# Where a slot of split weights begins: 192 bytes further for the down products, 128 bytes for the u units

## What is computed

```
merged = sum_i gate_i * (o_i @ w_proj_i);  x = x + merged @ w_out                  # w_out: "down"
x = x + square(relu(h @ w_mlp_in)) @ w_mlp_out                                     # "up", "down"
swiglu(x, w1, w3, w2) = (silu(x @ w1) * (x @ w3)) @ w2                             # four of them: "up", "up", "down"
u, v = split(gelu(x @ sgu_w_in));  out = (u * mix(layer_norm(v))) @ sgu_w_out      # gating stage: u, v "up"; "down"
out = attention(...) @ w_o                                                         # "down"
```

## Time and profile before

| | |
|---|---|
| runs | 1498.37, 1498.73, 1499.16 us; median 1498.73 us |
| profiled execution | 1499.37 us, span of its instructions 1497.5 us |
| TensorE matmul busy | 1445.4 us, 97% of the span |
| TensorE weight loads busy | 1326.4 us, 89% |
| VectorE, ScalarE, GpSimd busy | 62%, 44%, 6% |
| TensorE clock granted | 0.987 of full, mean |
| DMA | 268.43 MB, 179 GB/s |

### The profile page before, as it was taken

One profiled execution on the slowest core, in us unless ns is written; L12 is line 12 of the kernel. 1 busy time (PEld: TensorE's weight loads), 2 busy tenths in 40 slices (PEclk: granted clock), 3 DMA queues, 4 the chain that ended last, 5 costly groups with the idle time before them and its releaser, 6 DMA issues.

```text
span 1497.5 us, 25321 instructions
## 1 busy us (share of the span) xinstructions
PE 1445.4 (97%) x10475; PEld 1326.4 (89%) x10484; DVE 930.4 (62%) x1363; ACT 660.1 (44%) x834; POOL 95.9 (6%) x78
## 2 busy tenths in 40 slices
PE   8989998999999999999999999999999998999997
PEld 6978987899999999999789999999999886799996
DVE  5887457555675555757885555746555767665556
ACT  5655534333444434545244334425334466543342
POOL 0012141000020000100020000100000100100000
PEclk9999998999999999999999999999999999999999
DMA  7443444776568555665356556667555440455551
GB/s 256 150 141 95 146 142 155 219 218 212 193 222 284 185 188 191 198 195 196 113 178 204 187 193 196 198 195 250 179 190 196 147 141 29 141 198 196 196 196 57
DMA packets 191526, 268.43 MB, mean 179 GB/s; under 512 B 5740, under 2 KB 164752, under 8 KB 191182
## 3 DMA queue, kind: packets, MB, share of 16 engines
q1 hardware_dynamic: 186336, 250.05, 51.2%
q0 software_dynamic: 4224, 15.91, 3.2%
q10 hardware_dynamic: 878, 1.21, 0.3%
HBM read 261.92 MB, written 4.19 MB: 178 GB/s over the span
## 4 chain that ended last, share of the span: by engine, by line
PE 84%; DVE 9%; ACT 3%; DMA 2%; issue 1%; POOL 0%; DVEq 0%; ACTq 0%
PE bank L764 82%; DVE split L2024 2%; DMA ring<-in_ffn_w 2%; PE bank L787 2%; ACT split L1553 1%; DVE resid L2101 1%; DVE resid L2109 1%; DVE stats L2080 1%; DVE resid L2078 1%; ACT act_out L1576 0%; DVE arena L2616 0%; DVE stats L2038 0%; DVE arena L2221 0%; ACT gain_rows L1680 0%; DMA resid<-in_x 0%
## 5 line engine op out<-in xcount | busy, mean ns | idle before, releaser
L764 PE MATMUL bank<-hT_hi,split 128*128 128x256 f32 (+1 forms) x3984 | 710.7, 280 | 7.5 <-ACT act_out L1692 5.4
L2024 DVE TENSOR_TENSOR split<-ring,split 128x2048 fp32r<-128x2048 f32 x212 | 484.3, 2286 | 369.1 <-ACT split L1553 363.8
L764 PEld LDWEIGHTS bank<-hT_hi,split 128*128 128x128 f32 (+1 forms) x3984 | 613.8, 189 | 16.0 <-issue 9.8
L1553 ACT ACTIVATE split<-ring 128x2048 fp32r<-128x2048 f32 (+1 forms) x224 | 428.1, 1912 | 352.9 <-PE bank L764 313.7
L764 PE MATMUL bank<-hT_lo,split 128*128 128x256 f32 (+1 forms) x1992 | 556.5, 279 | 0.0
L764 PEld LDWEIGHTS bank<-hT_lo,split 128*128 128x128 f32 (+1 forms) x1992 | 376.3, 189 | 2.0
L764 PE MATMUL bank<-split,hid_hi 128*128 128x512 f32 x992 | 286.2, 395 | 0.0
L764 PEld LDWEIGHTS bank<-split,hid_hi 128*128 128x128 f32 x992 | 183.3, 189 | 37.7 <-issue 0.8
L764 PE MATMUL bank<-split,hT_hi 128*128 128x256 f32 (+1 forms) x896 | 174.1, 294 | 6.5 <-DVE split L2024 4.8
L764 PE MATMUL bank<-split,hid_lo 128*128 128x512 f32 x496 | 158.3, 393 | 0.0
L764 PEld LDWEIGHTS bank<-split,hT_hi 128*128 128x128 f32 x896 | 141.5, 189 | 14.4 <-DVE split L2024 5.4
(11 more groups left out here) (216 smaller groups left out, 964.5 us busy)
## 6 DMA issues: line engine op xcount, KB each, us to landing
ring<-in_ffn_w SPq DMA_DIRECT2D x132, 1024.0 KB, 5.1
ring<-in_w_in SPq DMA_DIRECT2D x19, 1024.0 KB, 5.1
ring<-in_w_mlp_in SPq DMA_DIRECT2D x16, 1024.0 KB, 6.2
ring<-in_w_mlp_out SPq DMA_DIRECT2D x16, 1024.0 KB, 4.9
ring<-in_sgu_w_in SPq DMA_DIRECT2D x16, 1024.0 KB, 5.4
ring<-in_sgu_w_out SPq DMA_DIRECT2D x8, 1024.0 KB, 4.9
ring<-in_kv_w SPq DMA_DIRECT2D x6, 1024.0 KB, 5.4
ring<-in_w_out SPq DMA_DIRECT2D x4, 1024.0 KB, 4.9
```

What stands on the lines that cost most here:

```text
L764: ins = pe.matmul(o, lhsT, rhs, start=start, stop=stop)
L1553: act.activation(halves(q if i is None else q + BODY, n)[0], ring[:, u % SLOTS, 0:n], ACT.Copy).then_inc(hi_ready, 1)
L2024: dve.tensor_tensor(lo, ring[:, u % SLOTS, 0:n], hi.bitcast(F32), ALU.subtract).then_inc(split_ready, 1)
```

## The change

Units of the down products lie 48 floats (192 bytes) further in their slot (at 384 modulo 512 in place of 192), the `su` units 32 floats (128 bytes; at 320 in place of 192). Units of `by_token` keep their 32, all others their 0. The last unit of each down stage lies in `two` and does not move.

```diff
+SHIFTS = {"wout": 3 * SHIFT // 2, "md": 3 * SHIFT // 2, "w2": 3 * SHIFT // 2, "so": 3 * SHIFT // 2, "wo": 3 * SHIFT // 2,
+          "mu": 0, "w1": 0, "w3": 0, "sv": SHIFT, "su": SHIFT}
+
+
 def split_shift(q):
 
-    return SHIFT if by_token(SPLIT_NAMES[q]) else 0
+    name = SPLIT_NAMES[q]
+    if by_token(name) and name[0] != "sv":
+        return SHIFT
+    return SHIFTS.get(name[0], 0)
```

## The result

The change makes the kernel slower: 1509.19 us (median of 5 runs, 1508.76 to 1512.06) against 1498.73 us before (5 runs of the same comparison); the ratio is 1.0075, with a 95% interval of 1.005 to 1.010: small, but clear of the noise. In later comparisons the kernel before had a median of 1496.5 to 1499.4 us over 13 to 29 runs. The profiled execution of the changed kernel took 1512.06 us, with a span of 1510.3.

The account below looks back on a forecast made before the run. It took TensorE's dense matmuls (97% busy) as the bound. Down units (-5.4 us) and su units (-1.6 us), other terms 0, sum to -7.0 us from 1499.37: 1492 us for the median, 8-in-10 range 1481 to 1507.

Parts of the forecast that it names:

- What bounds the kernel: Whole kernel: TensorE's matmuls, busy 97% of the span, bound it, so a nanosecond per matmul goes to the end whole.
- Slot passes at nothing: VectorE's and ScalarE's writing of the slots: costs the same at either shift, and both engines have slack; term 0.
- The su units, -1.6 us: Gating stage: 384 su matmuls go from 117.8 to 113.6 ns, as sv at the same 192 bytes apart; 1.6 us won.
- The down units, -3.3 ns each: 68 down units, 1632 matmuls at about 229 ns: each gets 3.3 ns shorter at offset 384, 5.4 us won.
- The analogy with 256 columns: Down units: the 4.3 ns between sv at shift 32 and memory values at 0 was taken over for 512 columns.
- The up units behind down units, term 0: MLP and FFNs: addresses stay; 7.3 us to win or 12.1 us to lose, nothing to say which, so 0.
- The third rival: Up units lock slow: three fast FFNs run at 117.8 ns, +12.1 us, less 5.4 and 1.6 won: 1504 us; chance 0.18.
- its second price, 1509 us: Three fast FFNs' up units at 117.8 ns, with no gain in the down units: 1509 us.
- more than forecast: Rival: a constant down rhythm makes all following up units fast, 1484 us, or most of 13 ns goes, 1478; chance 0.17.
- It stays at one for a whole stage: TensorE's timeline: the same instruction comes at two or three steady distances (113.6 or 117.8, 229 or 233 ns), one per stage.
- The rule of the Trainium skill: TensorE has two independent SBUF read ports, so no offset would change a distance and the change would be worth 0.
- The first 200 us as before to the nanosecond: Test of the prediction: the first 200 us hold no moved unit, so each distance there must be unchanged.

Follow-up runs that it names:

- the nudge: The changed kernel plus one bf16 matmul of zeros (64 columns), adding nothing, ahead of each FFN chunk's w1 unit from the third chunk on: 1499.07 us, ratio 1.0011.
- the kernel with lo at 64: The changed kernel, with only the down units' first part (hi) at 48 floats and the second (lo) at 64: 1513.45 us, ratio 1.0102.
- the one with 64 floats: The changed kernel, with the down units 64 floats (256 bytes) further in place of 48, at 448 modulo 512: 1492.60 us, ratio 0.9985.

## Why the prediction was wrong

The forecast was 1492 us; the time is 1509.19, beyond the range's 1507.

- *What bounds the kernel* held. Of the 12.8 us by which the profiled span grew, 3.7 arose ahead of the first moved unit and 1.9 in the second attention stage; nearly all of the rest are distances between matmuls.
- *Slot passes at nothing* held: around the first FFN VectorE's took 2293 ns, ScalarE's 1918 ns on average.
- *The su units, -1.6 us*: right in size, -1.7 us in the profile (113.3 ns). The reason given, 192 bytes between the operands as with sv, is not enough: the w1, w3 and mu units at 320, as far from their moving operand, ran at 117.8 behind another stream.
- *The down units, -3.3 ns each*: the sign was right, the size wrong. It was -1.1 ns where the up units were short before and -2.0 where they were long. The even rhythm of the unit in `two` did come (226.7 ns when settled), but each down unit spends its first five matmuls at 227 to 237 ns, behind long and short up units alike. The analogy with 256 columns was worth nothing.
- *The up units behind down units, term 0*: this is the step that failed. They carried the sign. Three FFNs went from 113.6 to 117.8 ns, 4.2 ns x 96 = 0.40 us a chunk, up to 12.1 us in all. In the traces the three FFNs show 8.6 us of it, net of what their down units won, in 8, 9 and 9 pairs of up units. The third rival had this mechanism and its price; what I lacked was its probability. That its second price, 1509 us, is the measured time is luck: it puts the gain of the down units at nothing, which was 1.1 to 2.0 ns a matmul.

And it could have been read from the trace of before. I used the even rhythm of the earlier trace rows for the size of the down term, but did not ask how such a rhythm hands over. In the stages of before with long up units (MLP, third FFN) these were entered at 226 to 227 ns in all 22 hand-overs, in those with short ones at 230 to 231 in all of 26. An even rhythm of 226 to 227 can only leave at 226 to 227. By these rows, to forecast that rhythm was to forecast long up units in every stage, and my rival "more than forecast" had it the wrong way round. They were a hint and no proof: at the old offset long up units and a last distance of 227 may just as well keep each other up.

Smaller points:

- *"It stays at one for a whole stage"* misread the rows. The down unit of 233.3 ns lies between 96 up matmuls at 118.9 ns and the short ones: it is where the first FFN turned.
- *The unit in `two`*: 1.81 us / 8 is 226.3 ns, not 226.5; nothing hangs on it.
- *The rule of the Trainium skill* ("TensorE: Matmul & The Clock Gate", Part 2 on the steps of a matmul: the next load of weights takes no read bandwidth from the running matmul). The measurements decide against its consequence here: with the moving operand's address the average distance of the same 512-column matmuls changes, behind short up units from 228.9 ns (192 and 448) to 227.9 (384, with the nudge), 232.4 (256) and 232.9 (320). Whether it is the two reads that meet, or something else that depends on the address, no run here shows.
- *The first 200 us as before to the nanosecond*: wrong as a test. Nothing was moved there, and the one profiled execution came 3.7 us later than the other.

**What stays open.** Why 227 ns leads to the one distance and 228 to the other; the last distance is a mark of the phase, and it was not shown that it is the phase's cause. Nor what decides, at the old offset, which way the MLP and the third FFN go in an execution; a stretch with waits lies ahead of each. Nor why su's own address decides behind sv, and that of w1, w3 and mu did not behind down units at 384. An offset with both an even down rhythm and short up units was not found; a nudge that costs no weight load was not tried.

## What to carry to other kernels

Where TensorE runs dense with a weight load for every matmul, measure start-to-start distances, per stage, before and after moving any buffer; busy times hide them. Treat the steady distance as a state with memory: judge an operand's new address by the stage that follows it as well, whose matmuls may be four times as many. Where one kernel shows two distances for the same instructions, look for what differs at the entrance of the stage, and vary that with the addresses held.

## What the runs showed of the hardware that was not expected

- Matmuls of 256 float32 columns with a load of 128 settle at one of two distances, 113.3 or 117.8 ns, at TensorE's full granted clock, and keep it over hundreds of matmuls; 384 in a row in su.
- Behind down units it was decided at the hand-over, with a sharp edge between 227 and 228 ns in 576 cases of 60 stages.
- A down unit with its hi part at 384 handed over to long up units whatever was ahead of it (short up units in eleven cases); at 192 it mostly kept what it found.
- Behind the same sv units, su took 117.8 ns at 192 and 113.3 ns at 320, in two and in twelve profiles.
- Two pairs of addresses of the moving operand 256 bytes apart acted alike: 192 and 448 gave the same rhythm, 128 (`two`) and 384 the same even one.
- A matmul of 64 bf16 columns at the hand-over made the third start behind it 0.127 us later (230 + 39 + 202 ns where 226 + 118 stood), and the stretch of 96 matmuls still ended 0.28 us earlier.
- The same stage with the same addresses ran at either distance in different profiles, some 2.6 us apart for the MLP (14 units x 48 x 3.9 ns). It may be part of why the kernel before spreads from 1492.5 to 1507.8 us over all its runs, but that isn't shown: the kernel with lo at 64, long in its profile, spreads over 7.8 us in six runs, the one with 64 floats, short in its profile, over 9.9 us in ten.
